# One-core transformer kernel: modulation spread inside the per-layer input, squares of both modulated norms taken a stage sooner, attention's start regrouped

## What is computed

```python
# first block, attention: each head's scores are shifted by running sums c of log forget gates
log_f = jax.nn.log_sigmoid(f_logit + b_f)
c = jnp.cumsum(log_f, axis=1)
s = q @ k.T * scale + c[query] - c[key]          # then causal mask, softmax, times v
# end of the first block, the per-layer input
gate = jax.nn.sigmoid(x @ ple_w_gate + ple_b_gate)
x = x + gate * (p @ ple_w_proj)
# second block
mod = jax.nn.silu(c_2) @ w_ada + b_ada            # one row of 6 x 1024
shift1, scale1, gate1, shift2, scale2, gate2 = split(mod, 6)
h = x * rsqrt(mean(x * x) + eps) * norm1_w * (1 + scale1) + shift1
...
x = x + gate1 * (mixed @ w_out)
h2 = x * rsqrt(mean(x * x) + eps) * norm2_w * (1 + scale2) + shift2
```

## Time and profile before

| | |
|---|---|
| median of three runs | 3526.2 us |
| the profiled execution | 3523.97 us |
| its span | 3522.1 us |
| attention | 0 to 606 us |
| per-layer input | 1516 to 1683 us |
| modulation | 1683 to 1707 us |
| first modulated norm | 1707 to 1740 us |
| mix out | 2524 to 2651 us |
| second modulated norm | 2651 to 2686 us |
| experts | 2735 to 3475 us |

### The profile page before, as it was taken

The page is one execution under the profiler, slowest core; times in us unless marked ns, Lnnn a source line. Parts: engine busy times, 40 slices in busy tenths (PEclk is TensorE's granted clock), DMA queues, the critical chain, the costliest instruction groups (busy, mean ns, idle before and its releaser), DMA issues. The chain is left out here.

```text
span 3522.1 us, 40464 instructions
## 1 busy us (share of the span) xinstructions
PE 3103.1 (88%) x14608; PEld 2227.7 (63%) x14608; DVE 1535.7 (44%) x2012; ACT 1125.4 (32%) x1505; POOL 1110.3 (32%) x562
## 2 busy tenths in 40 slices
PE   6999999989999999769698997999594899999993
PEld 4666666468888788634343455999342677777772
DVE  4444444421111211336400334444415687878775
ACT  3333333011111122210210221222202677777773
POOL 1000110223333344400001213222000577878784
PEclk9999999999999999879799998999796899999996
DMA  2000001211111232145300004000303899999995
GB/s 86 24 25 19 25 25 59 91 47 52 50 48 48 77 119 93 57 185 179 146 24 23 30 31 174 13 13 1 124 9 123 286 372 371 368 368 375 365 375 214
DMA packets 116368, 450.06 MB, mean 128 GB/s; under 512 B 14609, under 2 KB 15569, under 8 KB 111265
## 3 DMA queue, kind: packets, MB, share of 16 engines
q1 hardware_dynamic: 103074, 396.83, 30.7%
q0 software_dynamic: 7856, 28.64, 2.4%
q10 hardware_dynamic: 5328, 23.07, 1.6%
HBM read 404.30 MB, written 44.10 MB: 127 GB/s over the span
## 5 line engine op out<-in xcount | busy, mean ns | idle before, releaser
L2685 DVE TENSOR_TENSOR moe_w_low<-moe_raw_up,moe_w_high 128x1024 fp32r<-128x1024 f32 x288 | 436.4, 1554 | 156.2 <-ACT moe_w_high L2625 156.2
L2548 POOL TENSOR_TENSOR moe_w_low<-moe_raw_down,moe_w_high 128x1024 fp32r<-128x1024 f32 x144 | 417.0, 2925 | 148.6 <-ACT moe_w_high L2635 148.6
L2625 ACT ACTIVATE moe_w_high<-moe_raw_up 128x1024 fp32r<-128x1024 f32 x288 | 304.9, 1062 | 187.5 <-PE ps L2588 110.3
L91 PE MATMUL ps<-x1T_high,w_up_high 128*128 128x512 f32 x704 | 274.7, 390 | 3.5 <-PEq L2906 3.5
L91 PE MATMUL ps<-x1T_low,w_up_high 128*128 128x512 f32 x704 | 274.3, 390 | 0.0
L91 PE MATMUL ps<-x1T_high,w_up_low 128*128 128x512 f32 x704 | 274.3, 390 | 0.0
L2603 PE MATMUL ps<-moe_w_high,moe_x_high 128*128 128x512 f32 x576 | 229.1, 398 | 4.2 <-DVE moe_x_low L2716 4.2
L2605 PE MATMUL ps<-moe_w_high,moe_x_low 128*128 128x512 f32 x576 | 226.0, 392 | 0.0
L2604 PE MATMUL ps<-moe_w_low,moe_x_high 128*128 128x512 f32 x576 | 225.6, 392 | 0.0
L764 POOL TENSOR_TENSOR w_up_high<-w_up,consts 128x1024 fp32r<-128x1024 f32 x44 | 83.5, 1897 | 382.7 <-PE ps L91 285.1
L272 POOL TENSOR_TENSOR qkv_low<-qkv_raw,qkv_high 128x1024 fp32r<-128x1024 f32 x22 | 53.6, 2436 | 468.3 <-ACT qkv_high L564 468.3
(11 more groups left out here) (433 smaller groups left out, 6147.4 us busy)
## 6 DMA issues: line engine op xcount, KB each, us to landing
moe_raw_up<-in_w SPq DMA_DIRECT2D x288, 512.0 KB, 10.2
moe_raw_down<-in_w SPq DMA_DIRECT2D x144, 512.0 KB, 9.1
w_ada<-in_w_ada SPq DMA_DIRECT2D x48, 512.0 KB, 4.6
w_up<-in_ffn_w_up SPq DMA_DIRECT2D x22, 1024.0 KB, 4.8
w_down<-in_ffn_w_down SPq DMA_DIRECT2D x44, 512.0 KB, 3.5
y_rows<-xT ACTq DMA_DIRECT2D x36, 512.0 KB, 8.2
qkv_raw<-in_attn_w SPq DMA_DIRECT2D x22, 512.0 KB, 3.5
y_rows<-zero_rows SPq DMA_DIRECT2D x1, 8192.0 KB, 29.1
```

Source lines behind the costliest of these rows:

```text
L91: ins = pe.matmul(out, stationary, moving, start=start and n == 0, stop=stop and n == last)
L2548: pool.tensor_tensor(w_low[:, down_slot(k)], raw_down[:, k], w_high[:, down_slot(k)].bitcast(F32), ALU.subtract).then_inc(down_low, 1)
L2625: act.activation(w_high[:, up_slot(n)], raw_up[:, n], ACT.Copy).then_inc(up_high, 1)
L2685: dve.tensor_tensor(w_low[:, up_slot(n)], raw_up[:, n], w_high[:, up_slot(n)].bitcast(F32), ALU.subtract).then_inc(up_low, 1)
```

## The change

In the attention the gate's product and the carry's product come one k sooner; the copies to negc are split over three queues: part 0 and half of part 2 on SP, part 1 on ScalarE, the other half of part 2 on POOL; the first unit's pieces are moved ahead of the wait for them. In the per-layer input four products of w_ada are taken in each of the first 12 halves, with the row b_ada loaded into partition 0 of m.mod, which POOL has cleared; the 12 products with ones are put in the last four halves, three each, ScalarE copies them out, and VectorE folds in the norm weights at the last two halves. Three pairs of PSUM banks are used for the halves instead of four. stage_modulation is gone. The squares move to ScalarE's lists of stage_per_layer_input and of stage_mix_out, and their sums to tensors that outlive the stage. The diff, cut to its core:

```diff
+        def spread_part(eng, j, c, landed):
+            for head in range(2):
+                row = 64 * head + j
+                eng.dma_start(negc[row:row + 1, :, c * FCHUNK:(c + 1) * FCHUNK],
+                              parts[c * THIN + head:c * THIN + HEADS:2, j, :]).then_inc(landed, 16)
...
+            sp.wait_ge(parted, 2)
+            for c in range(TILES):
+                spread_part(sp, 0, c, spread)
             sp.wait_ge(parted, 6)
-            for j in range(3):
-                for head in range(2):
-                    row = 64 * head + j
-                    for c in range(TILES):
-                        sp.dma_start(negc[row:row + 1, :, c * FCHUNK:(c + 1) * FCHUNK],
-                                     parts[c * THIN + head:c * THIN + HEADS:2, j, :]).then_inc(spread, 16)
+            for c in range(TILES // 2):
+                spread_part(sp, 2, c, spread)
...
+            pool.wait_ge(parted, 6)
+            for c in range(TILES // 2, TILES):
+                spread_part(pool, 2, c, spread_pool)
...
-                if k == 3:
+                if k == 2:
...
-                if k == 6:
+                if k == 5:
...
-            pe.wait_ge(spread, 16 * 6 * TILES)
+            for n in pieces(0):
+                piece(0, n)
+            pe.wait_ge(spread, 16 * 3 * TILES)
+            pe.wait_ge(spread_act, 16 * 2 * TILES)
+            pe.wait_ge(spread_pool, 16 * TILES)
             for u in range(UNITS):
-                fill = pieces(u)
+                fill = pieces(u) if u else []
...
+            act.wait_ge(parted, 4)
+            for c in range(TILES):
+                spread_part(act, 1, c, spread_act)
...
-        PER_HALF = STEPS // (2 * TT)
+        PER_HALF = 4
+        ADA_HALVES = STEPS // PER_HALF
+        MOD_CHUNKS = N_MOD * NH
+        PER_LATE_HALF = MOD_CHUNKS // (NH * TT - ADA_HALVES)
+        SLOTS_PLE = 3
...
+            sp.wait_ge(cleared, 1)
+            sp.dma_start(m.mod[0:1, :], d["b_ada"].partition_broadcast(1)).then_inc(b_loaded, 16)
+            sp.dma_start(nw[:, 0, :], d["norm1_w"].partition_broadcast(P)).then_inc(norm_w_loaded, 16)
+            sp.dma_start(nw[:, 1, :], d["norm2_w"].partition_broadcast(P)).then_inc(norm_w_loaded, 16)
...
+            pool.memset(m.mod[:], 0.0).then_inc(cleared, 1)
...
+            def spread_mod(j):
+                pe.wait_ge(ada[j // NH], DT)
+                if j >= 2:
+                    pe.wait_ge(mod_out, j - 1)
+                pe.matmul(ps[:, 6 + j % 2, :], m.ones[:], m.mod[:, j * HALF:(j + 1) * HALF],
+                          start=True, stop=True).then_inc(mod_summed, 1)
...
+                    late = PER_LATE_HALF * (i - ADA_HALVES)
+                    if i >= SLOTS_PLE:
+                        pe.wait_ge(scaled, i - SLOTS_PLE + 1)
                     group(pe, ps[:, b, :], [(m.xT[:, k, rows], w[:, n, k, :]) for k in range(DT)])
+                    if late >= 0:
+                        spread_mod(late)
+                        spread_mod(late + 1)
                     group(pe, ps[:, b + 1, :], [(pT[:, k, rows], wp[:, k, cols]) for k in range(PLE // P)]
                           ).then_inc(summed, 1)
+                    if late >= 0:
+                        spread_mod(late + 2)
...
+            def mod_copy(j):
+                act.wait_ge(mod_summed, j + 1)
+                act.activation(m.mod[:, j * HALF:(j + 1) * HALF], ps[:, 6 + j % 2, :], ACT.Copy
+                               ).then_inc(mod_out, 1)
+            def square_tile(t):
+                act.wait_ge(added, NH * (t + 1))
+                if t:
+                    act.wait_ge(squared, t)
+                act.activation(square[:], m.res[:, t, :], ACT.Square, accum_out=m.norm1_ss[:, t:t + 1]
+                               ).then_inc(squared, 1)
             for i in range(NH * TT):
+                late = PER_LATE_HALF * (i - ADA_HALVES)
+                if late >= 0:
+                    mod_copy(late)
+                    mod_copy(late + 1)
                 act.wait_ge(biased, i + 1)
                 act.activation(z[:, i % 2], z[:, i % 2], ACT.Sigmoid).then_inc(gated, 1)
+                if late >= 0:
+                    mod_copy(late + 2)
+                if i >= NH and i % NH == 0:
+                    square_tile(i // NH - 1)
+            square_tile(TT - 1)
...
-                    dve.tensor_scalar(acc, wa[:, n, :], c[:, 0:1], None, ALU.mult).then_inc(ada[n], 1)
+                    dve.wait_ge(b_loaded, 16)
                 else:
                     dve.wait_ge(ada[n], k)
-                    dve.scalar_tensor_tensor(acc, wa[:, n, :], c[:, k:k + 1], acc, ALU.mult, ALU.add
-                                             ).then_inc(ada[n], 1)
+                dve.scalar_tensor_tensor(acc, wa[:, n, :], c[:, k:k + 1], acc, ALU.mult, ALU.add
+                                         ).then_inc(ada[n], 1)
+            def norm_scale(j):
+                scale = m.mod[:, (3 * j + 1) * D:(3 * j + 2) * D]
+                dve.wait_ge(norm_w_loaded, 32)
+                dve.wait_ge(mod_out, NH * (3 * j + 2))
+                dve.scalar_tensor_tensor(scale, scale, 1.0, nw[:, j, :], ALU.add, ALU.mult)
             for i in range(NH * TT):
                 t, n = i // NH, i % NH
-                b = 2 * (i % 4)
+                b = 2 * (i % SLOTS_PLE)
                 cols = slice(n * HALF, (n + 1) * HALF)
+                if i == NH * TT - 2:
+                    norm_scale(0)
+                if i == NH * TT - 1:
...
+                    norm_scale(1)
...
-                for j in range(PER_HALF * i, PER_HALF * (i + 1)):
-                    ada_product(j)
+                if i < ADA_HALVES:
+                    for j in range(PER_HALF * i, PER_HALF * (i + 1)):
+                        ada_product(j)
...
-def stage_modulation(nc, d, m):
-    with ExitStack() as ctx:
-        b = ctx.enter_context(nc.sbuf_tensor("b_ada", [P, N_MOD * D], F32))
-        nw = ctx.enter_context(nc.sbuf_tensor("norm_w", [P, 2, D], F32))
-        loaded, summed, added = (nc.alloc_semaphore(n)
-                                 for n in ("mod_loaded", "mod_summed", "mod_added"))
-        CH = N_MOD * D // HALF
-        block = ctx.enter_context(nc.Block())
...
-            for t in range(TT):
-                if t:
-                    act.wait_ge(squared, t)
-                act.activation(square[:], m.res[:, t, :], ACT.Square, accum_out=ss[:, t:t + 1]
-                               ).then_inc(squared, 1)
...
-            dve.wait_ge(squared, TT)
...
+            for t in range(TT):
+                act.wait_ge(added, NH * (t + 1))
+                if t:
+                    act.wait_ge(squared, t)
+                act.activation(square[:], m.res[:, t, :], ACT.Square, accum_out=m.norm2_ss[:, t:t + 1]
+                               ).then_inc(squared, 1)
...
-                stage_modulation(nc, d, m)
```

More of the change, by code:

```diff
@@ L172, in stage_attention @@
         halves = sem("halves_ready")
+        spread_act, spread_pool = sem("f_spread_act"), sem("f_spread_pool")
         qk_bank, qk_out, filled, fill_out = sem("qk_bank"), sem("qk_out"), sem("filled"), sem("fill_out")
@@ L263, in _ @@
                 sp.dma_start(m.w_attn_out[:, n], d["attn_w_out"][n]).then_inc(m.w_attn_out_loaded, 16)
-            sp.wait_ge(spread, 16 * 6 * TILES)
+            sp.wait_ge(spread, 16 * 3 * TILES)
         @block.gpsimd
@@ L1034, in stage_per_layer_input @@
         wa = sb("w_ada", [P, N_MOD, D])
+        nw = sb("norm_w", [P, 2, D])
+        square = sb("norm1_square", [P, D])
         loaded, p_loaded, c_loaded = sem("ple_loaded"), sem("ple_p_loaded"), sem("c_loaded")
@@ L1058, in _ @@
                     sp.dma_start(wa[:, n, :], d["w_ada"][k, n]).then_inc(a_loaded[n], 16)
+        @block.gpsimd
+        def _(pool):
+            pool.memset(m.mod[:], 0.0).then_inc(cleared, 1)
         @block.tensor
         def _(pe):
+            def spread_mod(j):
[4 more added lines that the diff above has]
+                          start=True, stop=True).then_inc(mod_summed, 1)
             pe.wait_ge(p_loaded, 48)
@@ L1117, in _ @@
                                   ).then_inc(added, 1)
-def stage_modulation(nc, d, m):
-    with ExitStack() as ctx:
-        b = ctx.enter_context(nc.sbuf_tensor("b_ada", [P, N_MOD * D], F32))
-        nw = ctx.enter_context(nc.sbuf_tensor("norm_w", [P, 2, D], F32))
-        loaded, summed, added = (nc.alloc_semaphore(n)
-                                 for n in ("mod_loaded", "mod_summed", "mod_added"))
-        CH = N_MOD * D // HALF
-        block = ctx.enter_context(nc.Block())
-        @block.sync
-        def _(sp):
-            sp.dma_start(b[:], d["b_ada"].partition_broadcast(P)).then_inc(loaded, 16)
-            sp.dma_start(nw[:, 0, :], d["norm1_w"].partition_broadcast(P)).then_inc(loaded, 16)
-            sp.dma_start(nw[:, 1, :], d["norm2_w"].partition_broadcast(P)).then_inc(loaded, 16)
-        @block.tensor
-        def _(pe):
-            for j in range(CH):
```

(26 more changed lines are left out.)

6 lines of the change are left out of this document (3 added, 3 removed).

## The result

The changed kernel took 3479.1 us (median of four runs, 3477.42 to 3485.04), against 3526.13 us for the kernel before (3525.41 to 3530.25). The ratio is 0.9867, with an interval of 0.9853 to 0.9882: a gain of 47.0 us where 45.1 were forecast. The profiled execution took 3477.42 us, its span 3475.6; it was the fastest of the four.

A forecast was written before the change was run, and what follows sets the result against it. TensorE is busy 88%, so gains come only from real gaps or other engines' lone work between barriers. 15.5+15.8+6.8-1.3+8.3 = 45.1 us off the profiled 3523.97 gives 3478.9, plus 2.2 for the median: 3481.1 us; range 3475 to 3492.

The forecast's parts named there:

- Attention: Attention's start: earlier casts, copies split over three queues and V pieces in the hole gain 15.5 us.
- The landing: Attention's start: ScalarE's last small copy lands 1.87 us after its issue, so scores start at 46.6.
- Per-layer input: Per-layer input and modulation: spreading modulation into the halves starts the first norm 15.8 us earlier.
- Late halves: Per-layer input: last four halves take 11.2 us each; 11 added products put 9.5 us on the path.
- clearing: Per-layer input's start: POOL clears 6144 columns in nothing to 14 us, hidden, so it costs nothing.
- First norm: First modulated norm: squares leave, the res_rows transfer becomes the end, 26.7 us instead of 33.5; gain 6.8.
- rival 3: First norm not held by its transfer: all 9.5 us come, TensorE stays warm, total 3477; chance 6%.
- Clock behind the norm: Stage behind the first norm: TensorE's longer barrier wait costs clock, between nothing and 2.6 us; taken as -1.3.
- Second norm: Second norm: squares moved behind the mix's additions bring the first DVE step 8.3 us sooner.
- Issues of ScalarE and SP add up: Attention's copies: the two queues take turns issuing, last copy lands at 49.4, 2.8 us later, total 3484; chance 12%.
- POOL's copies land last: Attention's copies: POOL's land at up to 53.5 instead of 46.6, 6.9 us given back, total 3488; chance 8%.
- The single w_ada buffer: Per-layer input: load, product and issue exceed 12.9 us, costing from 11.2 us landing; slower than before from 17.6; chance 2%.

The follow-up runs named there:

- Experiment 4: Changed kernel with none of the 24 negc copies on ScalarE: SP issues 10, POOL 14; 3476.17 us.
- Experiment 2: Kernel before with only modulation spread in the per-layer input; both norms keep their squares, attention as before; 3509.87 us.
- experiment 7: Changed kernel with the first unit's four V pieces behind its scores again, copies still on three queues; 3484.66 us.
- Experiment 11: Changed kernel with the second norm's eight squares back in that norm's stage; 3485.64 us.
- experiment 1: Kernel before with the attention part of the change alone; 3512.95 us.
- experiment 6: Changed kernel with the first norm's eight squares back in that norm's stage; 3485.71 us.
- experiment 3: Changed kernel with seven of the eight res_rows stores issued in the per-layer input, before the first norm stage; 3481.39 us.
- experiment 10: Changed kernel with two more mod_row stores, each waited for, behind the first norm stage's waits; 3483.13 us.
- the same again (5): The changed kernel run again with nothing changed; 3478.94 us.
- both (8): Changed kernel with seven res_rows stores in the per-layer input and no negc copies on ScalarE; 3474.89 us.
- experiment 9: Changed kernel with one more mod_row store, waited for, behind the first norm stage's waits; 3480.14 us.

## Why the prediction was right

The mechanisms held, but for the reason given for the clock; several terms were mis-sized, and the total is as near as it is partly by luck. By its steps, against the profiled execution:

- **Attention, 15.5 forecast, 13.3 measured.** The mechanism was right: the last cast ends at 36.42 (36.08 forecast), ScalarE's queue decides, the V pieces end at 45.05 (44.8). Two terms were mis-sized. The landing: ScalarE's last issue starts at 45.04 (44.7 forecast), but the scores start 2.7 us behind it where 1.87 was assumed, 47.78 instead of 46.6. The 1.87 came from a copy with little beside it; the change also lets SP issue the next 512 KB of weights ahead of ScalarE's last copies, which now travel beside them. The sum had no term for that. That the weights are the cause is read from the traces; that ScalarE's queue is slower by itself was not excluded. And it charged no clock here: V's transposes come at 50.84, a gain of 65.51-50.84 = 14.7, and by unit 2 the slower products have brought the gain down to 13.5. Experiment 4 took both down together.
- **Per-layer input, 15.8 and 15.8.** Late halves 11.16 us (11.2 forecast); VectorE waits for no w_ada load; clearing 5.22 us, between the bounds of nothing and 14, and hidden. Experiment 2 isolates the part.
- **First norm, 6.8 and 6.7.** The transfer does become the end, and rival 3 is dead. But both sides of the comparison were mis-sized, and the match is partly luck. The 26.7 us is the long end of what this transfer takes: five kernels or executions without added waits have stages of 26.8, 25.3, 25.4, 25.4 and 25.6 us (the changed kernel twice, experiments 4, 7 and 11). Compute needs 24.9 us and not 24.0: the 33.5 from which 9.5 was taken had its last tile's transposes at 2.4 GHz (1.09 us), and the changed kernel has them at 1.2 GHz (1.95 us). So the hold is 0.4 to 1.9 us, mostly about 0.5. The row of one execution was taken for the price.
- **Clock behind the norm, -1.3 forecast.** 6.13 us for what took 5.09: -1.04, near the forecast, but the step's reason, that a longer wait costs clock, is not borne out. (Its bound also has a slip: 6.19-3.44 is 2.75, not 2.6.) With an idle of 1.37 us ahead, the same 64 instructions took 3.66 us in experiments 1 and 6, 5.12 in experiment 2 and 6.41 in experiment 3; after 6.08 us of idle (experiment 10) they took 6.40. The stretch that begins with them came out 2.3 us shorter all the same, so 3.3 us were won in code that nobody changed. That was in no step, and it is why the total exceeded the forecast although the attention fell short. They go with the granted clock: see below.
- **Second norm, 8.3 and 8.2.** Experiment 11 gives the 8.2 back.

The sum by the profile is 13.3+15.8+6.7+2.3+8.2+0.2 = 46.5 us, the difference of the spans. The forecast's 45.1 came as near as it did by luck: a shortfall of 2.2 and a windfall of 3.6 (2.3 instead of -1.3) nearly cancel.

**The rivals.** *Issues of ScalarE and SP add up*: from 39.65 to 42.6 both issue, SP at a pitch of 8.39/12 = 0.70 us as before, and ScalarE's eight take 0.63 us each but for one of 1.28; the scores started at 47.78, short of the rival's 49.4. The Trainium skill ("Perfetto Trace Analysis", section "DMA Instruction — HWDGE (DVE, Sync)") has the generator locked for one sequencer at a time. The trace agrees with that for at most one issue, and by the whole time it does not. *POOL's copies land last*: they cost 0.52 us each and landed in 1.6 us, where the gathers had suggested 1.80 and 4.6; POOL is the first to be done. In experiment 4, with 14 copies, it is POOL's that land last, at up to 3.5 us. The Trainium skill's 2.0 us fixed ("DMA: Bandwidth & Descriptors", section "Anatomy of one DMA") was nearer than my row. *The single w_ada buffer*: the median landing was 4.9 us, far from 11.2.

**Why unchanged stretches differ.** The feed-forward stretch, from the load of its taps to the per-layer input, takes 777 to 780 us and the one from row projection to mix 803 to 807 us, from one program to another. The traces record the granted clock, and the time for which it stood at 1.2 GHz can be added up over each stretch:

| | feed-forward, us | of it at 1.2 GHz | row projection to mix, us | of it at 1.2 GHz |
|---|---|---|---|---|
| kernel before | 777.0 | 44.4 | 805.9 | 84.9 |
| changed kernel | 777.2 | 44.7 | 803.6 | 80.1 |
| the same again (5) | 776.9 | 44.4 | 804.0 | 81.6 |
| stores early (3) | 779.2 | 50.8 | 806.5 | 84.1 |
| no copies on ScalarE (4) | 780.1 | 54.3 | 807.3 | 84.9 |
| V behind the scores (7) | 777.1 | 44.5 | 802.9 | 78.0 |
| both (8) | 778.1 | 45.9 | 806.6 | 85.5 |

Over all thirteen traces the two columns of a stretch have a correlation of 0.98 for the feed-forward part and of 0.85 for the other. The place where experiment 4 loses its 2.9 us can be seen in the windows: the same two pieces of the feed-forward stretch in the changed kernel and in experiment 4 (third column from the end: granted clock):

```profile
1210.50:1225.50 15.00, 11.71 (x43) 9.56 (x44) 3.62 (x3) 2.82 (x4) 5.12 (x2) 0.77 0.99 397
1230.00:1245.00 15.00, 15.00 (x67) 12.40 (x67) 1.39 (x2) 3.17 (x4) 6.73 (x3) 1.00 0.34 106
```

```profile
1206.50:1221.50 15.00, 10.32 (x34) 8.28 (x35) 3.76 (x3) 3.67 (x5) 5.12 (x2) 0.66 0.92 361
1226.00:1241.00 15.00, 14.18 (x56) 11.59 (x57) 2.43 (x3) 3.58 (x5) 5.73 (x3) 0.89 0.32 98
```

The changed kernel's windfall of 2.3 us goes with a clock that stood at 1.2 GHz for 4.8 us less than before, in code that it did not change; by the slope of a line through the thirteen points, 0.46 us per us, that is worth an estimated 2.2 us. No run sets the clock, so this is a correlation and not a test.

**What stays open.** It is not settled what makes the clock stay low for longer in one program than in another. The same program repeated its stretches within 0.4 us. Experiments 9 and 10 show that the start has some part in it (1.7 us), experiments 8 and 11 that it doesn't settle it.

## What to carry to other kernels

When work is taken out of a stage that ends in a barrier, read the DMA queue's own waits first: the stage can lose no more than down to its slowest transfer, and that transfer's time varies from one execution to the next, so it is worth a range and not one row. Small copies whose issue is the price belong on the queue that is free when their data is ready, POOL's too; the one engine that has evictions to do first decides. Look also at what each queue issues next: a large load that comes sooner can make the last small copies land later. Work that is due anyway is best put ahead of a wait instead of behind it. When the total misses and the local gain is there, compare the granted clock over the stretches that the edit does not touch before looking for another cause.

## What the runs showed of the hardware

- POOL issued copies of this kind in 0.50 to 0.58 us each, less than SP (0.635) and ScalarE (0.63, the first 1.28). Landing took 1.6 us, but up to 3.5 us beside a load of 512 KB (experiment 4).
- An idle of 0.88 to 0.96 us at the attention's start left TensorE at full clock (experiments 8 and 4, four score instructions 0.49 us). After 2.6 to 2.8 us of idle it differed between executions: 0.80 us in the changed kernel and experiments 1 and 6, 0.67 in the changed kernel's second execution, 0.49 us in experiments 9, 10 and 11, where the clock fell only behind the scores, at 49.6 to 49.8 us. Experiment 11:

```profile
47.44 0.49 PE L335 MATMUL ps<-qk 64*128 64x128 f32 x4 [2.84 <-issue]
```

- POOL cleared 128x6144 float32 in 5.22 us.
- Two executions of one program differed by 1.7 us at the attention's exit and 1.5 us in the first norm, while the long TensorE stages repeated within 0.4 us; different programs with the same code in those stages differ by up to 3.2 us (feed-forward) and 4.4 us (row projection to mix: 802.9 in experiment 7, 807.3 in experiment 4).
